# Rows of the last tile pair spread over a whole dense loop, with one block in sixteen left free, and the split of the weights written ahead of the dot

## The chip, the cores and the metric

The kernel runs on one core of one Trainium2 chip. The metric is the device time of one execution in microseconds (us); the three runs of the kernel before gave 2140.74, 2141.62 and 2150.8 us. The engines are TensorE (PE), VectorE (DVE), ScalarE (ACT), GpSimd (POOL) and the queue of SyncE (SP), which here only issues DMAs.

## The reference, cut to what matters

One decoder layer for 512 prompt tokens and 8 sample tokens. A mixer stage comes first (its output is `h`); the change does not touch it. Then comes a layer of 16384 one-neuron experts:

```python
q = einsum('td,de->te', xb, w_q)                    # 8 heads x 2 halves x 128
s = einsum('thpd,hpkd->thpk', q, keys)              # scores against 128 keys per half
s_top, i_top = top_k(s, 16)                         # the best 16 of each half
best, sel = top_k(all 16 x 16 sums, 16)             # 16 experts per token and head
gate = softmax(best)
act  = gelu(einsum('td,thkd->thk', xb, u_tab[eidx]))
out  = einsum('thk,thkd->td', gate * act, v_tab[eidx])
```

The result is added to `h` and normalised.

## The kernel before

The tokens form four tiles of 128 (t = 0 to 3) and one of 8 sample tokens. For each token of a tile 8 x 16 = 128 experts are needed; fetching "row p" means fetching, for each of the 128 partitions, that token's p-th expert with one indirect DMA. There are two ways to get the activations.

**The paired way** (tile 0 and the sample tokens, rows p = 0 to 135; `HK` = 128 rows of tile 0, then 8 sample rows, `PAIRS` = 136). POOL's `gather_pair(p)` fetches U and V of the expert together (8 KB per partition, 1 MB in all) into a ring of `RING` = 7 slots. DVE's `dot(p)` multiplies U by x and sums. ACT's `row(p)` applies Gelu and the gate to the 128 sums. Then V is added: for tile 0 by DVE's `add_vector(p)` into `ex_fin`, for sample rows by PE's `add_row(p)`. The slot is free after that.

**The dense way** (tiles 1 to 3). PE multiplies all of U by x in 128 "z" blocks of 128 experts; 16 "q" blocks make the queries. These 144 blocks (`expert_blocks`: blocks 0 to 112 are seven units of 16 blocks, of which the first and the fourth are q blocks, then z blocks alone) form the **dense loop**. In step i of it:

- SP loads block i+3 (512 KB) into one of three buffers `ex_w_raw` once the `lower` of block i is done, and stores the finished z block i-1 to `value_rows` in DRAM.
- ACT does `activate(i-1)` (Gelu out of PSUM into `ex_z_rows`; for q blocks two `take`), which waits for PE's block i-1; then `upper(i+2)` (the high half `ex_w_hi` of the weights), which waits for the load; then `row(p)`, which waits for `dot(p)`; in one step of a unit also `weight(u)` (an Exp, for which the activation table is changed twice).
- DVE does `dot(p)`, then `lower(i+2)` (the low half `ex_w_lo` = raw - high), which waits for `upper(i+2)`, then `add_vector(p-1)`, which waits for `row(p-1)`. In four steps of a unit (9, 11, 13, 15) it also does a quarter of `retrieve`, the two top-k of the next unit.
- PE does block i with 24 (z) or 48 (q) matmuls once `lower(i)` is done, and behind it `add_row` of a sample row, if there is one.

Each engine runs its list in the order in which it is written, and the engines meet only at semaphores. Row p stands in step p + `ROWS_FROM` = p + 8, so rows 0 to 135 fill steps 8 to 143, one in each.

Behind the dense loop the **value phase** handles 384 rows of tiles 1 to 3. `gather_value` fetches from `value_rows` (V beside the activations) through `VALUES` = 10 slots that lie on top of the seven pair slots: its first gather waits for all pair gathers ahead of it on POOL's queue, for the last store of `value_rows`, and for the pair rows in the slots below it. DVE's `picked` forms a diagonal of coefficients and PE's `add_row` adds V; a quarter of the rows goes through DVE's `add_vector`. Ahead of the first `picked` DVE has `scale(0)`, which waits for ACT's `root(0)`, and `normalise`.

Of the kernel before, what the change touches and what calls it, by code (L numbers as in the profile page):

```python
# [60 lines left out]
TOPK = 16  # L61
# [5 lines left out]
HK = PH * TOPK  # L67
# [6 lines left out]
WROW = D + BT  # L74
VALUE_SLOT = D + 2 * P
VALUES = 10
ROWS_FROM = 8
SPREADS = 6
PARTS_AT = (1, 4, 7, 10)
VECTOR_LAST = 1  # L80
# [1751 lines left out]
def experts(k, a, o, x_hi, x_lo, x_first, h_store, again, q, keys, keysT, h_tok, gains_row, h_out, uv_row):  # L1832
# [10 lines left out]
    PAIRS = HK + PER_ROW  # L1843
# [7 lines left out]
    blocks = expert_blocks()  # L1851
# [2 lines left out]
    by_vector = {*range(HK), *(rests - late), *range(SLOTS - VECTOR_LAST, SLOTS)}  # L1854
    rows_upto = lambda p, kind: sum((m in by_vector) == kind for m in range(p))
    on_tensor, on_vector = ([rows_upto(p, kind) for p in range(SLOTS + 1)] for kind in (False, True))
    retrieve_at, scores_at, weight_at, normalise_at = unit_schedule(SAMPLE)
    with ExitStack() as ctx:
        sb = lambda n, s, dt=F32: k.sb("ex_" + n, s, dt, ctx)
# [102 lines left out]
        with nc.Block() as block:  # L1962
# [120 lines left out]
            def _(pe):  # L2083
# [89 lines left out]
                for i, (kind, n) in enumerate(blocks):  # L2173
                    if kind == "q":
                        queries(i, n)
                    else:
                        activities(i, n)
                    if i in scores_at:
                        scores(scores_at[i])
                    if HK <= i - ROWS_FROM - 1 < PAIRS:  # L2180
                        add_row(i - ROWS_FROM - 1)
                for p in range(len(blocks) - ROWS_FROM - 1, PAIRS):
                    add_row(p)
                scores(PH + 2)
                for p in range(PAIRS, SLOTS):
# [7 lines left out]
            def _(act):  # L2193
# [86 lines left out]
                for i, (kind, n) in enumerate(blocks):  # L2280
                    if i and blocks[i - 1][0] == "z":
                        activate(blocks[i - 1][1])
                    elif i:
                        take(blocks[i - 1][1], 0)
                        take(blocks[i - 1][1], 1)
                    if i and i + 2 < len(blocks):
                        upper(i + 2)
                    if 0 <= i - ROWS_FROM < PAIRS:
                        row(i - ROWS_FROM)
                    if i in weight_at:  # L2290
                        weight(weight_at[i])
                activate(NE // P - 1)
                for p in range(len(blocks) - ROWS_FROM, PAIRS):
                    row(p)
                root(0)
                root(1)
# [10 lines left out]
            def _(dve):  # L2307
# [61 lines left out]
                def dot(p):  # L2369
                    n = order[p]  # L2370
                    if p == HK:
                        dve.wait_ge(x_in, 16 * NS)
                    dve.wait_ge(pair_loaded[p % RING], 16 * (p // RING + 1))
                    u = uv_row[:, p % RING, 0:D]
                    x = x_first[:, :] if n < HK else x_rep
                    dve.tensor_tensor_reduce(u, u, x, 1.0, 0.0, ALU.mult, ALU.add, coef[:, n:n + 1]).then_inc(dotted, 1)  # L2376
# [88 lines left out]
                lower_x(4)  # L2465
                retrieve(0)
                for i in range(len(blocks)):
                    p = i - ROWS_FROM
                    if 0 <= p < PAIRS:
                        dot(p)  # L2470
                    if 5 <= i + 2 < len(blocks) and by_dve(i + 2):
                        lower(dve, i + 2)
                    if 0 < p <= HK:
                        add_vector(p - 1)
                    if p == HK:
                        add(0)
                    if i in retrieve_at:
                        retrieve(*retrieve_at[i])
                    if i in normalise_at:
                        normalise(normalise_at[i])  # L2480
                for p in range(len(blocks) - ROWS_FROM, PAIRS):
                    dot(p)
                scale(0)
                normalise(PH + 1)
                for p in range(PAIRS, SLOTS):
# [144 lines left out]
```

## Time and profile before

| | |
|---|---|
| median of three runs | 2141.62 us (2140.74 to 2150.8) |
| the profiled execution | 2143.07 us, its span 2141.0 us |
| busy over the span | PE 90%, DVE 63%, ACT 29%, POOL 32% |
| dense loop, last activation of a z block | 1531.45 us |
| value phase, first gather | 1535.00 us |

The profile is of one execution on this core. The page gives busy shares over the whole span. The timeline has one line per instruction: start, duration, engine, line, what is written from what, and in brackets how long the engine sat idle before it and what ended that. The windows view gives busy time of each engine in a stretch, the granted clock of PE, the busy share of the DMA engines and what they moved.

### The profile page before, as it was taken

The numbers are of one execution on the slowest core, as the hardware profiler recorded it, in microseconds if no ns is written. First come the engines' busy times: TensorE is split into PE (matmuls) and PEld (weight loads), VectorE is DVE, ScalarE is ACT, GpSimd is POOL, SyncE is SP. The second block draws the span as 40 slices with busy tenths as digits, with TensorE's granted clock in tenths as the row PEclk, the third lists the DMA queues.
The fourth block names the chain that finished last, engine by engine and source line by source line (L and its number), as shares of the span: only waits on it lengthen the run. The fifth ranks groups of instructions, "written<-read, shape, count | busy, mean of one in ns | idle before, by whom it ended". The sixth has DMA issues, their size and how long they took to land.

```text
span 2141.0 us, 29757 instructions
## 1 busy us (share of the span) xinstructions
PE 1934.9 (90%) x10912; PEld 1564.2 (73%) x10912; DVE 1358.9 (63%) x2860; ACT 616.4 (29%) x1217; POOL 675.5 (32%) x556
## 2 busy tenths in 40 slices
PE   5998889988996988999999999998899998999886
PEld 4997889978966988998999999998544433434332
DVE  3219263353345535488988888988377777776663
ACT  4223312252224324444445444445300000000000
POOL 0003012100000000232333233232277776776663
PEclk9999899988998999999999999999999999999999
DMA  3557158637614573899999999999499999999997
GB/s 117 197 198 220 31 180 260 216 86 257 237 41 178 177 261 119 318 366 349 403 388 361 388 394 357 376 364 376 184 412 403 404 407 412 397 398 415 405 414 290
DMA packets 244650, 629.25 MB, mean 294 GB/s; under 512 B 19714, under 2 KB 137541, under 8 KB 226712
## 3 DMA queue, kind: packets, MB, share of 16 engines
q0 software_dynamic: 74880, 377.52, 44.5%
q1 hardware_dynamic: 169632, 249.92, 34.4%
q8 instruction: 83, 1.36, 0.2%
q14 instruction: 55, 0.45, 0.1%
HBM read 584.36 MB, written 110.21 MB: 324 GB/s over the span
## 4 chain that ended last, share of the span: by engine, by line
DMA 19%; PE 15%; DVE 14%; issue 7%; ACT 2%; POOL 2%; SPq 1%; DVEq 1%; another core or an unknown queue 0%; ACTq 0%; POOLq 0%
DMA ex_w_raw<-in_peer_ut 10%; DMA ex_uv_row<-value_rows,ex_eidx 9%; PE ps L2137 9%; DVE ex_fin L2388 4%; DVE ex_w_lo L1935 3%; POOL ex_uv_row L2066 2%; PE ps L589 2%; PE ps L590 2%; PE ps L591 2%; DVE ex_uv_row L2376 2%; ACT ex_w_hi L2199 1%; DVE ex_q_s L2401 1%; DVE ex_top_i L2335 0%; SPq L1989 0%; DVEq L162 0%
## 5 line engine op out<-in xcount | busy, mean ns | idle before, releaser
L2137 PE MATMUL ps<-ex_uv_row,ex_q_s 128*128 128x512 f32 (+1 forms) x1208 | 542.4, 599 | 61.3 <-DVE ex_q_s L2401 47.3
L2137 PEld LDWEIGHTS ps<-ex_uv_row,ex_q_s 128*128 128x128 f32 (+1 forms) x1208 | 217.1, 187 | 366.3 <-issue 347.6
L2066 POOL DMA_INDIRECT ex_uv_row<-value_rows,ex_eidx x384 | 405.2, 1055 | 214.6 <-issue 102.2
L589 PE MATMUL ps<-x_hi,ex_w_lo 128*128 128x384 f32 (+2 forms) x1296 | 427.6, 330 | 27.8 <-DVE ex_w_lo L1935 22.6
L590 PE MATMUL ps<-x_lo,ex_w_hi 128*128 128x384 f32 (+2 forms) x1296 | 423.6, 327 | 0.0
L591 PE MATMUL ps<-x_hi,ex_w_hi 128*128 128x384 f32 (+2 forms) x1296 | 423.5, 327 | 0.0
L2050 POOL DMA_INDIRECT ex_uv_row<-in_peer_uv,ex_eidx x128 | 190.6, 1489 | 410.2 <-DVE ex_fin L2388 404.7
L2388 DVE SCALAR_TENSOR_TENSOR ex_fin<-ex_uv_row,ret_tables,ex_fin 128x1024 f32<-128x1024 f32 x218 | 278.7, 1279 | 0.3
L589 PEld LDWEIGHTS ps<-x_hi,ex_w_lo 128*128 128x128 f32 x1296 | 244.6, 189 | 40.7 <-DVE ex_w_lo L1935 30.7
L591 PEld LDWEIGHTS ps<-x_hi,ex_w_hi 128*128 128x128 f32 x1296 | 245.0, 189 | 0.0
L590 PEld LDWEIGHTS ps<-x_lo,ex_w_hi 128*128 128x128 f32 x1296 | 244.8, 189 | 0.0
L1935 DVE TENSOR_TENSOR ex_w_lo<-ex_w_raw,ex_w_hi 128x1024 fp32r<-128x1024 f32 x141 | 172.3, 1222 | 102.0 <-ACT ex_w_hi L2199 93.3
L2199 ACT ACTIVATE ex_w_hi<-ex_w_raw 128x1024 fp32r<-128x1024 f32 x144 | 152.4, 1058 | 168.2 <-DMA ex_w_raw<-in_peer_ut 153.1
L2401 DVE SCALAR_TENSOR_TENSOR ex_q_s<-ex_uv_row,ret_tables,square 128x128 f32<-128x128 f32 x294 | 100.1, 352 | 90.0 <-DMA ex_uv_row<-value_rows,ex_eidx 41.7
L2376 DVE CUSTOM_DVE_ANT_0 ex_uv_row<-ex_uv_row,x_first 128x1024 f32<-128x1024 f32 x128 | 156.1, 1220 | 1.5 <-DVE ex_eidx L2361 0.3
L2217 ACT ACTIVATE ret_tables<-ex_best,ex_shift 128x16 f32<-128x16 f32 (+1 forms) x33 | 10.2, 308 | 483.6 <-DVE ex_eidx L2361 460.0
L589 PE MATMUL ps<-proj_b_whi,x_lo 128*128 128x256 f32 (+1 forms) x320 | 90.9, 284 | 7.8 <-DVE proj_b_wlo L498 7.0
L591 PE MATMUL ps<-proj_b_whi,x_hi 128*128 128x256 f32 (+1 forms) x320 | 90.6, 283 | 0.0
L590 PE MATMUL ps<-proj_b_wlo,x_hi 128*128 128x256 f32 (+1 forms) x320 | 90.4, 283 | 0.0
L643 POOL TENSOR_TENSOR dp_w_lo<-dp_w_raw,dp_w_hi 128x1024 fp32r<-128x1024 f32 x14 | 33.9, 2427 | 171.5 <-ACT dp_w_hi L669 171.5
L1935 POOL TENSOR_TENSOR ex_w_lo<-ex_w_raw,ex_w_hi 128x1024 fp32r<-128x1024 f32 x3 | 7.1, 2379 | 243.9 <-ACT ex_w_hi L2199 243.9
L2212 ACT ACTIVATE ex_z_rows<-ps 128x384 f32<-128x384 f32 x128 | 63.0, 492 | 39.4 <-PE ps L591 36.0
(415 smaller groups left out, 3418.5 us busy)
## 6 DMA issues: line engine op xcount, KB each, us to landing
value_rows<-in_peer_uv SPq DMA_DIRECT2D x64, 1024.0 KB
ex_w_raw<-in_peer_ut SPq DMA_DIRECT2D x128, 512.0 KB
value_rows<-ex_z_rows SPq DMA_DIRECT2D x128, 128.0 KB
first_raw<-in_w_in SPq DMA_DIRECT2D x8, 1024.0 KB, 7.9
ex_w_raw<-in_peer_wq SPq DMA_DIRECT2D x16, 512.0 KB
value_rows<-ex_z_rows SPq DMA_DIRECT2D x128, 64.0 KB
dp_w_raw<-in_w_in SPq DMA_DIRECT2D x14, 512.0 KB
ex_uv_row<-value_rows,ex_eidx POOLq DMA_INDIRECT x384
```

The source lines that it names most:

```text
L589: pe.matmul(out, left(llo, c), right(rhi, c), start=(c == 0), stop=False)
L590: pe.matmul(out, left(lhi, c), right(rlo, c), start=False, stop=False)
L591: ins = pe.matmul(out, left(lhi, c), right(rhi, c), start=False, stop=(c == kc - 1))
L1935: eng.tensor_tensor(w_lo[b][:, :, :], w_raw[b][:, :, :], w_hi[b][:, :, :].bitcast(F32), ALU.subtract).then_inc(split_v if by_dve(i) else s ...
L2050: pool.indirect_dma_start(uv_row[:, p % RING, :], None, a["peer_uv"][0], bass.IndirectOffsetOnAxis(ap=index, axis=0)).then_inc(pair_loaded ...
L2066: pool.indirect_dma_start(value_slot(p)[0], None, k.value_rows, bass.IndirectOffsetOnAxis(ap=eidx[:, u, n % TOPK:n % TOPK + 1], axis=0), e ...
L2137: ins = pe.matmul(k.pv[j % 2][0:r, c, :], spread[:, on_tensor[p] % SPREADS, 0:r], v[:, c * 512:(c + 1) * 512], start=first, stop=last)
L2199: act.activation(w_hi[b][:, :, :], w_raw[b][:, :, :], ACT.Copy).then_inc(rounded, 1)
L2212: act.activation(z_rows[:, b % DEEP, :], k.pb[b % 2][:, 0:BT], ACT.Gelu).then_inc(z_made, 1)
L2376: dve.tensor_tensor_reduce(u, u, x, 1.0, 0.0, ALU.mult, ALU.add, coef[:, n:n + 1]).then_inc(dotted, 1)
L2388: dve.scalar_tensor_tensor(fin[:, j % 2, :], v, coef[:, n:n + 1], fin[:, j % 2, :], ALU.mult, ALU.add).then_inc(vector_done, 1)
L2401: dve.scalar_tensor_tensor(spread[:, on_tensor[p] % SPREADS, :], z, gate_of(n), k.eye, ALU.mult, ALU.mult).then_inc(diagonal, 1)
```

## The change

It does four things. `ROWS_FROM` goes from 8 to 6. Steps 16, 32, ... 128 get no row (`row_at` maps a step to its row), so 130 rows stand in the loop and rows 130 to 135 behind it; of the sample rows PE adds only row 128 in the loop's last step and rows 129 to 135 behind it. Inside a DVE step `lower(i+2)` now comes ahead of `dot(p)`. The loops behind the dense loop start at `beside` = 130, with guards for cases in which tile 0's rows would reach that far.

```diff
-ROWS_FROM = 8
+ROWS_FROM = 6
...
+    row_at = dict(zip((i for i in range(ROWS_FROM, len(blocks)) if i % TOPK), range(PAIRS)))
+    beside = len(row_at)
...
-                    if HK <= i - ROWS_FROM - 1 < PAIRS:
-                        add_row(i - ROWS_FROM - 1)
-                for p in range(len(blocks) - ROWS_FROM - 1, PAIRS):
+                    if row_at.get(i, 0) > HK:
+                        add_row(row_at[i] - 1)
+                for p in range(max(HK, beside - 1), PAIRS):
                     add_row(p)
...
-                    if 0 <= i - ROWS_FROM < PAIRS:
-                        row(i - ROWS_FROM)
+                    if i in row_at:
+                        row(row_at[i])
...
-                for p in range(len(blocks) - ROWS_FROM, PAIRS):
+                for p in range(beside, PAIRS):
                     row(p)
...
-                    p = i - ROWS_FROM
-                    if 0 <= p < PAIRS:
-                        dot(p)
+                    p = row_at.get(i, -1)
                     if 5 <= i + 2 < len(blocks) and by_dve(i + 2):
                         lower(dve, i + 2)
+                    if p >= 0:
+                        dot(p)
                     if 0 < p <= HK:
                         add_vector(p - 1)
...
-                for p in range(len(blocks) - ROWS_FROM, PAIRS):
+                for p in range(beside, PAIRS):
                     dot(p)
+                    if p <= HK:
+                        add_vector(p - 1)
+                    if p == HK:
+                        add(0)
                 scale(0)
```

DVE's list in the middle of the dense loop before. L2376 is `dot`, L1935 `lower`, L2388 `add_vector`, L2353 and on the last quarter of `retrieve`:

```order
L2376 ISA ex_uv_row,ret_tables<-ex_uv_row,x_first 128x1024
L2376 ISA ret_tables 128x1
L1935 TENSOR_TENSOR ex_w_lo<-ex_w_raw,ex_w_hi 128x1024
L2388 SCALAR_TENSOR_TENSOR ex_fin<-ex_uv_row,ret_tables,ex_fin 128x1024
L2353 TENSOR_SCALAR ex_pick<-ex_sel 128x16
```

The same place now (the lines are two further down: L1937 `lower`, L2378 `dot`, L2390 `add_vector`; L2346 is the third quarter of `retrieve`):

```order
L1937 TENSOR_TENSOR ex_w_lo<-ex_w_raw,ex_w_hi 128x1024
L2378 ISA ex_uv_row,ret_tables<-ex_uv_row,x_first 128x1024
L2378 ISA ret_tables 128x1
L2390 SCALAR_TENSOR_TENSOR ex_fin<-ex_uv_row,ret_tables,ex_fin 128x1024
L2346 MAX ex_best<-ex_cand 128x8
```

`lower` and `dot` have changed places; ACT's list of a step (`activate`, `upper`, `row`) is as it was.

DVE's list at the end of the dense loop before, from its last `lower`; L2434 and L2435 are `scale(0)`:

```order
L1935 TENSOR_TENSOR ex_w_lo<-ex_w_raw,ex_w_hi 128x1024
L2376 ISA ex_uv_row,ret_tables<-ex_uv_row,ex_x_rep 128x1024
L2376 ISA ret_tables 128x1
L2376 ISA ex_uv_row,ret_tables<-ex_uv_row,ex_x_rep 128x1024
L2376 ISA ret_tables 128x1
L2434 RECIPROCAL ex_ms<-ex_ms 128x1
L2435 SCALAR_TENSOR_TENSOR ex_fin<-ex_fin,ex_ms,ex_w_raw 128x1024
```

And now, from its last `lower` on (x_first is the x of tile 0, ex_x_rep that of the sample rows; six more dots follow before `scale(0)`):

```order
L1937 TENSOR_TENSOR ex_w_lo<-ex_w_raw,ex_w_hi 128x1024
L2378 ISA ex_uv_row,ret_tables<-ex_uv_row,x_first 128x1024
L2378 ISA ret_tables 128x1
L2390 SCALAR_TENSOR_TENSOR ex_fin<-ex_uv_row,ret_tables,ex_fin 128x1024
L2378 ISA ex_uv_row,ret_tables<-ex_uv_row,ex_x_rep 128x1024
L2378 ISA ret_tables 128x1
L2390 SCALAR_TENSOR_TENSOR ex_fin<-ex_uv_row,ret_tables,ex_fin 128x1024
L2378 ISA ex_uv_row,ret_tables<-ex_uv_row,ex_x_rep 128x1024
L2378 ISA ret_tables 128x1
```

Where two dots followed the last `lower`, nine do now, and the last rows of tile 0 are added there too.

PE's list at that place before, and then now (L2137 and L2139 are `add_row`, two matmuls for each row; L2108 and L2110 are the scores of the next unit):

```order
L590 MATMUL ps<-x_lo,ex_w_hi 128x384
L591 MATMUL ps<-x_hi,ex_w_hi 128x384
L2137 MATMUL ps<-ex_uv_row,ex_q_s 8x512 x4
L2108 MATMUL ps<-keysT,q 128x128 x2
L2137 MATMUL ps<-ex_uv_row,ex_q_s 128x512 x30
```

```order
L590 MATMUL ps<-x_lo,ex_w_hi 128x384
L591 MATMUL ps<-x_hi,ex_w_hi 128x384
L2139 MATMUL ps<-ex_uv_row,ex_q_s 8x512 x16
L2110 MATMUL ps<-keysT,q 128x128 x2
L2139 MATMUL ps<-ex_uv_row,ex_q_s 128x512 x30
```

Six of the sample rows that PE had between blocks 137 and 143 now stand behind block 143, which makes eight there with the two that stood there before.

## Rows read from the trace of the kernel before

**Rows 1.** Windows: stretch, its length, busy us of each engine, clock, DMA share, GB/s.

```profile
937.10:1382.00 444.90, 431.71 (x2620) 426.78 (x2619) 387.21 (x600) 210.04 (x432) 144.94 (x97) 1.00 1.00 378
...
1535.00:2141.00 606.00, 534.86 (x1264) 226.84 (x1264) 429.85 (x1349) 22.48 (x63) 405.23 (x384) 0.99 0.99 394
```

**Rows 2.** Waits from 929 to 1531: who waited for whom, us in total, times, longest.

```profile
ACT ex_w_hi L2199 <- DMA ex_w_raw<-in_peer_ut: 133.7, 65, 6.7
ACT ret_tables L2224 <- DVE ret_tables L2376: 132.3, 78, 4.2
```

**Rows 3.** Timeline of ACT: `activate` of blocks 7, 17, 113 and 143.

```profile
887.97 0.48 ACT L2212 ACTIVATE ex_z_rows<-ps 128x384 f32<-128x384 f32 x1
...
937.09 0.49 ACT L2212 ACTIVATE ex_z_rows<-ps 128x384 f32<-128x384 f32 x1
...
1382.01 0.49 ACT L2212 ACTIVATE ex_z_rows<-ps 128x384 f32<-128x384 f32 x1
...
1531.45 0.49 ACT L2212 ACTIVATE ex_z_rows<-ps 128x384 f32<-128x384 f32 x1 [4.98 <-PE ps L591]
```

**Rows 4.** Timeline of DVE, two steps without retrieval.

```profile
1151.58 1.22 DVE L1935 TENSOR_TENSOR ex_w_lo<-ex_w_raw,ex_w_hi 128x1024 fp32r<-128x1024 f32 x1
1152.72 1.28 DVE L2388 SCALAR_TENSOR_TENSOR ex_fin<-ex_uv_row,ret_tables,ex_fin 128x1024 f32<-128x1024 f32 x1
1153.92 1.22 DVE L2376 CUSTOM_DVE_ANT_0 ex_uv_row<-ex_uv_row,x_first 128x1024 f32<-128x1024 f32 x1
...
1157.39 1.22 DVE L2376 CUSTOM_DVE_ANT_0 ex_uv_row<-ex_uv_row,x_first 128x1024 f32<-128x1024 f32 x1
...
1160.20 1.22 DVE L1935 TENSOR_TENSOR ex_w_lo<-ex_w_raw,ex_w_hi 128x1024 fp32r<-128x1024 f32 x1 [1.59 <-ACT ex_w_hi L2199]
```

**Rows 5.** Timeline of ACT in the same steps: `row`, `activate`, `upper`.

```profile
1151.70 0.20 ACT L2224 ACTIVATE ret_tables<-ret_tables 128x1 f32<-128x1 f32 x1 [3.97 <-DVE ret_tables L2376]
...
1152.26 0.49 ACT L2212 ACTIVATE ex_z_rows<-ps 128x384 f32<-128x384 f32 x1
1152.65 1.05 ACT L2199 ACTIVATE ex_w_hi<-ex_w_raw 128x1024 fp32r<-128x1024 f32 x1
...
1155.17 0.20 ACT L2224 ACTIVATE ret_tables<-ret_tables 128x1 f32<-128x1 f32 x1 [1.48 <-DVE ret_tables L2376]
...
1158.73 0.49 ACT L2212 ACTIVATE ex_z_rows<-ps 128x384 f32<-128x384 f32 x1
1159.12 1.05 ACT L2199 ACTIVATE ex_w_hi<-ex_w_raw 128x1024 fp32r<-128x1024 f32 x1
```

**Rows 6.** Timeline of DVE: `dot` at the ends of eight steps, four with retrieval.

```profile
1190.86 1.22 DVE L2376 CUSTOM_DVE_ANT_0 ex_uv_row<-ex_uv_row,x_first 128x1024 f32<-128x1024 f32 x1
...
1228.14 1.22 DVE L2376 CUSTOM_DVE_ANT_0 ex_uv_row<-ex_uv_row,x_first 128x1024 f32<-128x1024 f32 x1
```

**Rows 7.** Timeline of PE: two matmuls of a z block, three apart; a sample row.

```profile
1149.90 0.34 PE L589 MATMUL ps<-x_hi,ex_w_lo 128*128 128x384 f32 x1
...
1150.43 0.34 PE L589 MATMUL ps<-x_hi,ex_w_lo 128*128 128x384 f32 x1
...
1494.03 1.88 PE L2137 MATMUL ps<-ex_uv_row,ex_q_s 128*8 128x512 f32 x4
```

**Rows 8.** Timeline of SP and ACT: a load's issue, and the `upper` that waited for it.

```profile
1194.38 0.60 SPq L1983 DMA_DIRECT2D ex_w_raw<-in_peer_ut  x1
...
1205.21 1.06 ACT L2199 ACTIVATE ex_w_hi<-ex_w_raw 128x1024 fp32r<-128x1024 f32 x1 [2.95 <-DMA ex_w_raw<-in_peer_ut]
```

**Rows 9.** Timeline at the start of the value phase: `root(0)`, first gather, `normalise`, first `picked`.

```profile
1531.84 1.02 ACT L2238 ACTIVATE ps<-ex_fin 128x1024 f32<-128x1024 f32 x1
...
1535.00 1.98 POOL L2066 DMA_INDIRECT ex_uv_row<-value_rows,ex_eidx  x1 [37.76 <-PE ps L2137]
...
1536.28 0.23 DVE L2408 TENSOR_SCALAR ret_tables<-ret_tables,ex_tot 128x16 f32<-128x16 f32 x1
...
1541.92 0.35 DVE L2401 SCALAR_TENSOR_TENSOR ex_q_s<-ex_uv_row,ret_tables,square 128x128 f32<-128x128 f32 x1 [5.40 <-DMA ex_uv_row<-value_rows,ex_eidx]
```

## Prediction, made before the changed kernel ran

> **What bounds the kernel now.** I read the windows first, to see what a stretch is short of. The value phase lasts 606 us with the DMA engines at 0.99 and 394 GB/s [rows 1]: 384 rows in 606 us, 1.58 us each. Nothing in it changes, so it only starts earlier or later. What is left is the dense loop, up to the last `activate` at 1531.45 [rows 3]. In its six steady units of 16 blocks, from block 17 (937.09) to block 113 (1382.01), a unit takes 444.92 / 6 = **74.15 us** [rows 3]. In that stretch PE is busy 431.7 of 444.9 us, DVE 387.2, and the DMA share is 1.00 at 378 GB/s [rows 1]. So three resources are nearly full, and the waits say who waits for whom: ACT waits 133.7 us for loads of U and 132.3 us for the dot product [rows 2]. The period is thus set by how the lists of ACT and DVE mesh, with loads that come just late. That is where the change acts.
>
> **How a step runs now.** A plain DVE step is `dot` to `dot`, 1157.39 - 1153.92 = 3.47 us [rows 4]. A z block on PE takes 24 matmuls at (1150.43 - 1149.90) / 3 = 0.177 us, 4.2 us [rows 7]. With the dot first, `dot(p)` of a step is done while ACT still works on `upper(i+2)`: ACT finds it ready, goes on to `activate(i)`, and DVE's `lower` fits in beside that. A loop that goes from a dot through ACT to the next `lower` and back covers two steps, so it doesn't bind.
>
> **The order inside the step, the main term.** Now `lower(i+2)` stands ahead of `dot(p)`, on an engine that takes its list in order, and ACT's list is unchanged. That closes a ring of one step, every link of which waits for the last:
>
> - `activate(i-1)` to `upper(i+2)`: 1152.65 - 1152.26 = 0.39 [rows 5]
> - `upper` to `lower`: 1160.20 - 1159.12 = 1.08 [rows 4, 5]
> - `lower` to the next DVE instruction, now the dot: 1152.72 - 1151.58 = 1.14 [rows 4]
> - dot to ACT's `row`: 1155.17 - 1153.92 = 1.25 [rows 4, 5]
> - `row` to the next `activate`: 1152.26 - 1151.70 = 0.56 [rows 5]
>
> Together **4.42 us**. No step with a row can be shorter, whatever PE (4.2) and DVE (3.47) could do. `add_vector`, behind the dot, is beside it. What is lost with it: DVE falls behind in retrieval steps and today catches up at 3.47 us a step; now it can't. What is queued behind the waiting `lower` is the dot, and ACT waits for that.
>
> The retrieval steps stay DVE's own. Eight steps, four with retrieval, took 1228.14 - 1190.86 = 37.28 us [rows 6]; less four plain ones (13.9) and about 0.4 of waiting for `upper` leaves 22.9 us for the four. The step with `weight` adds the table changes to the ring: 1158.73 - 1155.17 = 3.56 from `row` to `activate` instead of 0.56 [rows 5], so 3.0 more, 7.4 us.
>
> **The step without a row.** It has no dot in its ring, so it could be as short as 0.39 + 1.08 = 1.5 us if PE is ahead and the load is in, and as long as a PE block, 4.2 us, if not. Nothing in the trace shows such a step in the middle. I take the middle, 2.9.
>
> **A unit now**: 10 plain steps 44.2, four retrieval steps 22.9, `weight` step 7.4, free step 2.9, and 0.7, an estimate for two q blocks, whose eviction is two instructions of a z block's kind. That is **78.1 us** (76.7 to 79.4 by the free step), against 74.15: +3.9 in each of six units, **+23.6** (+15.3 to +31.5).
>
> **The first and the last part.** From block 7 to 17 before: 937.09 - 887.97 = 49.1 us [rows 3]. Now 4 x 4.42 + 22.9 + 7.4 + 2.9 = 50.9: **+1.8** (+0.4 to +3.1). The two rows that move into steps 6 and 7 lie beside blocks where PE is the slower one and cost nothing; if not, 0.5 us. From block 113 to 143 before: 1531.45 - 1382.01 = 149.4 us [rows 3]. Now 11 retrieval steps (two full sets and one without its first quarter, about 63.1), three `weight` steps 22.2, a free step 2.9, 15 plain ones 66.3: 154.5, **+5.0** (+3.7 to +6.3). In it lies the gain of the moved sample rows: before, six blocks at the end carried 1.88 us of PE each [rows 7], 11.3 us. That time comes back only as far as the ring and the retrievals of steps 134 to 140 leave it, and these rows then run while the last store and the first value gathers are under way.
>
> **The tail.** Let X be the end of the last block. The value gathers still need the last store, 1535.00 - 1531.45 = 3.55 us after X [rows 3, 9]. POOL's gather of row 135 waits for row 128's slot, free at X + 1.9 (one sample row [rows 7]), and stands ahead of them: its 1 MB is 2.7 us at 394 GB/s. Its dot comes at about X + 1.9 + 6.9 + 1.1 = X + 9.9 (6.9 is gather to first use [rows 9], 1.1 an estimate for twice the bytes). Then dot 1.25, `row` of a sample row about 0.9, and `root(0)`, `scale(0)`, `normalise`, 1536.5 - 1531.84 = 4.7 [rows 9], all ahead of the first `picked`: X + 16.7, where it was 1541.92 - 1531.45 = 10.5. Ten value slots hold 15.8 us of transfers and hide most of these 6.2 us. I take the transfer alone, **+2.7** (0 to +6.2).
>
> **Loads.** DMA work per unit falls by one pair row of 1 MB, some 2.7 us of 74. On the other side, a load is issued after `lower` of three blocks earlier, and the ring leaves it 3 x 4.42 less `lower`, issue and `upper`, about 10.5 us; one took 1205.21 - 1194.38 = 10.8 us [rows 8]. If plain steps slip by 0.2 us for that, 79 steps give +16. If loads are in time, nothing. I take 0 for the sum and keep 16 as the upper end.
>
> The page "DMA: Bandwidth & Descriptors" of the Trainium skill, section on the anatomy of one DMA, fits a transfer as 2.0 us plus bytes over 436 GB/s. By that an estimate for a load is 3.2 us and none would ever be late; the trace doesn't agree, since [rows 8] show 10.8 us under this load. By the page the 16 us could be struck; by the row they stay.
>
> **Sum**: 23.6 + 1.8 + 5.0 + 2.7 = +33.1 us on a span of 2141.0, thus 2174.1, and 2176.2 for the profiled execution's 2143.07. The median before is 1.5 us below that execution, so against the runs I say **2175 us**. Its own range is 2161 (all low ends: +19.4) to 2205 (all high ends, +47, and the late loads, +16).
>
> **Rivals.**
> *Faster: loads and DVE were the limit, the order doesn't bind.* ACT's 133.7 us of waiting for loads [rows 2] speak for it: `lower` earlier means loads issued up to 1.2 us earlier, and a sixteenth of the gathers and dots goes. A unit would fall to PE's busy time, 431.71 / 6 = 72.0 us [rows 1]; six units give -12.9, the end up to -11.3 from the sample rows, the tail +2.7: -21.5, 2120 us. It decides if the ring comes out below 4.2 us, that is if `row` is done before ACT needs to go on; against it stand ACT's 78 waits for the dot already now [rows 2]. Chance 0.14.
> *No difference.* The ring binds, but free steps are worth a whole step and sample rows come back in full: 76.7 less some 1.5 of load waits a unit, +6, the end -6: within 11 us of before, 2131 to 2152. Chance 0.11.
> *Only the tail pays.* The dense loop is as before, since DMA at a share of 1.00 [rows 1] sets it in both; then +2.7 to +6.2, 2144 to 2148. That is within 0.5% too. Chance 0.05.
> *Slower, as summed*: 0.70.
>
> **How the numbers follow.** About 0.5% (11 us) is what this kernel's measurement can tell from no change. Slower 0.70; same 0.11 + 0.05 = 0.16; faster 0.14. The range leaves out the faster case and a little above: 2142 to 2205.
>
> **What would show it.** In the profile after, steps of 4.4 us one after another where there were 3.5 and 6; `lower` always waiting for `upper`; ACT's waits for the dot grown well over 132 us, its waits for loads shrunk; PE's waits for `ex_w_lo` grown; a unit near 78 us; eight sample rows behind block 143. A unit of 72 to 73 us would say that the ring has slack that I don't see; one above 80, that loads come late in it.

## The result, and the profile after

The changed kernel takes 2194.63 us (median of four runs, 2191.4 to 2197.2) against 2141.18 us for the kernel before (2125.25 to 2150.8). The ratio is 1.0256, 95% interval 1.0193 to 1.032: slower, inside the predicted range, but with 53 us of loss where 33 were forecast. Over all its runs here the kernel before lies between 2125.3 and 2158.4 us, so a few us of any difference between two profiles mean nothing. Ratios leave out the executions in a slower state of the chip, two of the kernel before (2796 and 3446 us) and one of run 11 (2149 us).

The profiled execution spans 2195.1 us. Cutting both spans at the same `activate` instructions shows where 54.1 us went. The starts after are these (ACT's timeline; L2214 is `activate`; blocks 7, 17, 113 and 143, as in [rows 3]):

```profile
893.17 0.49 ACT L2214 ACTIVATE ex_z_rows<-ps 128x384 f32<-128x384 f32 x1
...
946.03 0.49 ACT L2214 ACTIVATE ex_z_rows<-ps 128x384 f32<-128x384 f32 x1
...
1425.57 0.49 ACT L2214 ACTIVATE ex_z_rows<-ps 128x384 f32<-128x384 f32 x1
...
1578.62 0.47 ACT L2214 ACTIVATE ex_z_rows<-ps 128x384 f32<-128x384 f32 x1
```

| part | before | after | difference | forecast |
|---|---|---|---|---|
| up to the first `upper` of the dense loop | 828.6 | 830.7 | +2.1 | 0 |
| first `upper` to block 7 | 59.4 | 62.4 | +3.0 | 0 |
| block 7 to 17 | 49.1 | 52.9 | +3.8 | +1.8 |
| six units, block 17 to 113 | 444.9 | 479.5 | +34.6 | +23.6 |
| block 113 to 143 | 149.4 | 153.1 | +3.6 | +5.0 |
| block 143 to the end | 609.5 | 616.5 | +7.0 | +2.7 |

Each part is the difference of two starts. A unit is now 479.5 / 6 = 79.9 us, against 74.15.

**The ring.** One step after, in the order of time (ACT's and DVE's timelines; L2201 is `upper`, L1937 `lower`, L2378 `dot`, L2226 and L2231 `row`):

```profile
1107.59 1.07 ACT L2201 ACTIVATE ex_w_hi<-ex_w_raw 128x1024 fp32r<-128x1024 f32 x1
...
1108.70 1.23 DVE L1937 TENSOR_TENSOR ex_w_lo<-ex_w_raw,ex_w_hi 128x1024 fp32r<-128x1024 f32 x1 [0.76 <-ACT ex_w_hi L2201]
1109.84 1.22 DVE L2378 CUSTOM_DVE_ANT_0 ex_uv_row<-ex_uv_row,x_first 128x1024 f32<-128x1024 f32 x1
...
1111.10 0.20 ACT L2226 ACTIVATE ret_tables<-ret_tables 128x1 f32<-128x1 f32 x1 [2.43 <-DVE ret_tables L2378]
1111.33 0.29 ACT L2231 ACTIVATE ret_tables<-ret_tables 128x1 f32<-128x1 f32 x1
1111.66 0.49 ACT L2214 ACTIVATE ex_z_rows<-ps 128x384 f32<-128x384 f32 x1
1112.05 1.05 ACT L2201 ACTIVATE ex_w_hi<-ex_w_raw 128x1024 fp32r<-128x1024 f32 x1
```

Start to start the links are 1.11, 1.14, 1.26, 0.56 and 0.39, together 4.46 us from one `upper` to the next, where 4.42 was worked out. Both engines idle in each round: ACT 2.43 us for the dot, DVE 0.76 us for the high half. That is how a ring looks in a timeline: two engines take turns, each waiting for the other, and neither is full.

The waits (929 to 1578 us; who waited for whom, total, times, longest) say it for the whole loop:

```profile
ACT ret_tables L2226 <- DVE ret_tables L2378: 316.9, 121, 4.1
DVE ex_w_lo L1937 <- ACT ex_w_hi L2201: 130.9, 96, 3.9
...
PE ps L589 <- ACT ex_z_rows L2214: 57.5, 46, 4.5
ACT ex_w_hi L2201 <- DMA ex_w_raw<-in_peer_ut: 42.1, 28, 4.0
```

ACT's wait for the dot went from 132.3 to 316.9 us and its wait for loads from 133.7 to 42.1 [rows 2]. Loads did come sooner relative to their need, but nothing could use that. In the windows view of the six units (columns as in [rows 1]) everything is less full than it was: PE is busy 93% of the time (97% before), DVE 79% (87%), the DMA share is 0.95 (1.00), with 338 GB/s instead of 378:

```profile
946.00:1425.60 479.60, 444.84 (x2643) 427.82 (x2642) 378.02 (x586) 206.34 (x422) 87.25 (x90) 1.00 0.95 338
```

**The free step.** Around step 48, which has no row (ACT's timeline; the first `upper` is that of block 50, the second that of block 51; step 49 behind it is the one with `weight`):

```profile
1090.69 0.49 ACT L2214 ACTIVATE ex_z_rows<-ps 128x384 f32<-128x384 f32 x1
1091.18 1.06 ACT L2201 ACTIVATE ex_w_hi<-ex_w_raw 128x1024 fp32r<-128x1024 f32 x1
1092.15 0.47 ACT L2214 ACTIVATE ex_z_rows<-ps 128x384 f32<-128x384 f32 x1
1095.51 1.06 ACT L2201 ACTIVATE ex_w_hi<-ex_w_raw 128x1024 fp32r<-128x1024 f32 x1 [2.89 <-DMA ex_w_raw<-in_peer_ut]
...
1102.56 0.49 ACT L2214 ACTIVATE ex_z_rows<-ps 128x384 f32<-128x384 f32 x1
```

From `activate` to `activate` the free step is as short as it can be, 1092.15 - 1090.69 = 1.46 us, and the next `upper` then waits 2.89 us for its load. The two steps take 1102.56 - 1090.69 = 11.9 us, 12.4 on average over the six units, where 2.9 + 7.4 = 10.3 was forecast. Why was that load late? Its buffer was free after the `lower` of block 48, but SP's list has the store of block 46 ahead of it, and that store waits for ACT's `activate` (timelines of DVE, ACT and SP; L1990 is the first half of a store, L1985 a load):

```profile
1083.29 1.23 DVE L1937 TENSOR_TENSOR ex_w_lo<-ex_w_raw,ex_w_hi 128x1024 fp32r<-128x1024 f32 x1
...
1086.25 0.49 ACT L2214 ACTIVATE ex_z_rows<-ps 128x384 f32<-128x384 f32 x1
...
1086.77 0.33 SPq L1990 DMA_DIRECT2D value_rows<-ex_z_rows  x1
...
1087.72 0.57 SPq L1985 DMA_DIRECT2D ex_w_raw<-in_peer_ut  x1
```

The `lower` ends at 1084.52 and the load goes out at 1087.72, 3.2 us later; from there to the `upper` that waits for it are 7.8 us. So the ring reaches the loads too, through the stores. The order of SP's list was not varied, so what another order would give is not shown.

**The tail.** SP, POOL and DVE behind the last block, which ends at 1578.6 (L1991 is the second half of the last store, L2052 the gather of row 135, L2068 the first value gather, L2403 the first diagonal):

```profile
1578.96 1.47 POOL L2052 DMA_INDIRECT ex_uv_row<-in_peer_uv,ex_eidx_s  x1 [1.96 <-PE ps L2139]
...
1579.84 0.51 SPq L1991 DMA_DIRECT2D value_rows<-ex_z_rows  x1
...
1588.38 1.23 DVE L2378 CUSTOM_DVE_ANT_0 ex_uv_row<-ex_uv_row,ex_x_rep 128x1024 f32<-128x1024 f32 x1 [5.42 <-DMA ex_uv_row<-in_peer_uv,ex_eidx_s]
...
1588.99 1.43 POOL L2068 DMA_INDIRECT ex_uv_row<-value_rows,ex_eidx  x1 [8.55 <-issue]
...
1595.00 0.34 DVE L2403 SCALAR_TENSOR_TENSOR ex_q_s<-ex_uv_row,ret_tables,square 128x128 f32<-128x128 f32 x1
```

The first value gather starts 10.4 us behind the last block instead of 3.55 [rows 9], 9.15 us after the last store was issued; before, that took 1535.00 - 1532.35 = 2.65 us. "issue" means that the view names no releaser. What POOL's list has there is the wait for the last stores (PE's `add_row` of row 129, whose slot the first value gather needs, was done by about 1581). The DMA engines were carrying the pair gathers of rows 133 to 135, issued at 1572.68, 1575.02 and 1578.96, and the load of the last norm's gain, issued at 1578.84: 263 GB/s from 1579.8 to 1589.0, against 73 GB/s in the same wait before.

### The profile page after: what moved, and what is told of

Same layout as the page of the kernel before. It is cut to its first block, busy times and chain, and to the rows that moved or that the text cites. A ratio compares the mean times of both kernels' runs of the same rounds, so it can differ in the third digit from the quotient of the medians.

```text
span 2195.1 us, 29758 instructions
## 1 busy us (share of the span) xinstructions
PE 1952.7 (89%) x10912; PEld 1566.8 (71%) x10912; DVE 1363.8 (62%) x2860; ACT 615.6 (28%) x1217; POOL 611.3 (28%) x556
## 4 chain that ended last, share of the span: by engine, by line
DMA 21%; DVE 12%; issue 9%; PE 9%; ACT 7%; POOL 3%; SPq 2%; DVEq 0%; another core or an unknown queue 0%; POOLq 0%
DMA ex_w_raw<-in_peer_ut 11%; DMA ex_uv_row<-value_rows,ex_eidx 10%; PE ps L2139 7%; DVE ex_uv_row L2378 5%; ACT ex_w_hi L2201 3%; POOL ex_uv_row L2068 3%; DVE ex_fin L2390 2%; ACT ret_tables L2231 1%; ACT ex_z_rows L2214 1%; DVE ex_q_s L2403 1%; SPq L1991 1%; ACT ret_tables L2226 1%; DVE ex_top_i L2337 1%; ACT L2214 1%; PE ps L589 0%
## 5 line engine op out<-in xcount | busy, mean ns | idle before, releaser
L2139 PE MATMUL ps<-ex_uv_row,ex_q_s 128*128 128x512 f32 (+1 forms) x1208 | 541.3, 599 | 59.7 <-DVE ex_q_s L2403 43.0
L589 PE MATMUL ps<-x_hi,ex_w_lo 128*128 128x384 f32 (+2 forms) x1296 | 432.9, 334 | 65.4 <-ACT ex_z_rows L2214 62.0
L2139 PEld LDWEIGHTS ps<-ex_uv_row,ex_q_s 128*128 128x128 f32 (+1 forms) x1208 | 217.4, 187 | 367.6 <-issue 351.1
L2068 POOL DMA_INDIRECT ex_uv_row<-value_rows,ex_eidx x384 | 406.2, 1058 | 184.6 <-issue 112.2
L2052 POOL DMA_INDIRECT ex_uv_row<-in_peer_uv,ex_eidx x128 | 125.1, 977 | 555.3 <-DVE ex_fin L2390 547.2
L2390 DVE SCALAR_TENSOR_TENSOR ex_fin<-ex_uv_row,ret_tables,ex_fin 128x1024 f32<-128x1024 f32 x218 | 279.1, 1280 | 0.3
L1937 DVE TENSOR_TENSOR ex_w_lo<-ex_w_raw,ex_w_hi 128x1024 fp32r<-128x1024 f32 x141 | 172.6, 1225 | 163.0 <-ACT ex_w_hi L2201 160.5
L2201 ACT ACTIVATE ex_w_hi<-ex_w_raw 128x1024 fp32r<-128x1024 f32 x144 | 152.0, 1056 | 54.1 <-DMA ex_w_raw<-in_peer_ut 53.0
L2378 DVE CUSTOM_DVE_ANT_0 ex_uv_row<-ex_uv_row,x_first 128x1024 f32<-128x1024 f32 x128 | 155.9, 1218 | 0.0
L2403 DVE SCALAR_TENSOR_TENSOR ex_q_s<-ex_uv_row,ret_tables,square 128x128 f32<-128x128 f32 x294 | 99.9, 351 | 84.5 <-DMA ex_uv_row<-value_rows,ex_eidx 37.0
L2219 ACT ACTIVATE ret_tables<-ex_best,ex_shift 128x16 f32<-128x16 f32 (+1 forms) x33 | 10.2, 308 | 483.6 <-DVE ex_eidx L2363 483.5
L2226 ACT ACTIVATE ret_tables<-ret_tables 128x1 f32<-128x1 f32 x136 | 27.5, 202 | 344.5 <-DVE ret_tables L2378 344.5
L1937 POOL TENSOR_TENSOR ex_w_lo<-ex_w_raw,ex_w_hi 128x1024 fp32r<-128x1024 f32 x3 | 7.1, 2377 | 244.4 <-ACT ex_w_hi L2201 244.4
```

The costliest lines, as they stand in the source:

```text
L589: pe.matmul(out, left(llo, c), right(rhi, c), start=(c == 0), stop=False)
L1937: eng.tensor_tensor(w_lo[b][:, :, :], w_raw[b][:, :, :], w_hi[b][:, :, :].bitcast(F32), ALU.subtract).then_inc(split_v if by_dve(i) else s ...
L2052: pool.indirect_dma_start(uv_row[:, p % RING, :], None, a["peer_uv"][0], bass.IndirectOffsetOnAxis(ap=index, axis=0)).then_inc(pair_loaded ...
L2068: pool.indirect_dma_start(value_slot(p)[0], None, k.value_rows, bass.IndirectOffsetOnAxis(ap=eidx[:, u, n % TOPK:n % TOPK + 1], axis=0), e ...
L2139: ins = pe.matmul(k.pv[j % 2][0:r, c, :], spread[:, on_tensor[p] % SPREADS, 0:r], v[:, c * 512:(c + 1) * 512], start=first, stop=last)
L2201: act.activation(w_hi[b][:, :, :], w_raw[b][:, :, :], ACT.Copy).then_inc(rounded, 1)
```

## The experiments

The theory: the order inside DVE's step closes a ring of one step, and that is the loss; the rest is the tail and rows at steps 6 and 7. Rivals: the loss comes from where the rows stand (free steps with late loads, rows behind the loop), or DVE's order is bad in itself, by what it does to gathers and loads. A run's parts are cut at the same instructions as above. The runs were made in three series, in which the kernel before had medians of 2140.4 us (runs 1 to 4), 2142.3 (5 to 8) and 2139.6 (9 to 12); each ratio is against the kernel before of its own series, so across series ratios are compared and not times.

**1. The dot first again, all else as changed.**

```diff
-                    if 5 <= i + 2 < len(blocks) and by_dve(i + 2):
-                        lower(dve, i + 2)
                     if p >= 0:
                         dot(p)
+                    if 5 <= i + 2 < len(blocks) and by_dve(i + 2):
+                        lower(dve, i + 2)
```

> The changed kernel with the dot put back ahead of the lower half; the rows stay where the change put them. The ring theory (lower, dot, ACT's row, activate, upper, each waiting for the last, 4.42 us a step) says that this alone takes the loss away: a unit of 16 blocks at 72 to 73.5 us (before 74.15, less a row's work), the dense loop some 15 us shorter than before, the tail 7 us longer, about 2130 us. The rival, that the loss comes from where the rows stand (late loads behind free steps, rows behind the loop), says 2185 us or more and a unit near 79.9 us as in the changed kernel.

2122.96 us, ratio 0.992 (0.9893 to 0.9947): the order was the whole loss, and the placing of the rows is a gain. A unit is 72.7 us, from `activate` at 933.32 and 1369.43. The waits of this run (930 to 1530 us):

```profile
ACT ret_tables L2226 <- DVE ret_tables L2378: 132.5, 71, 4.8
ACT ex_w_hi L2201 <- DMA ex_w_raw<-in_peer_ut: 99.8, 53, 6.5
DVE ex_w_lo L1937 <- ACT ex_w_hi L2201: 77.0, 46, 5.6
```

The wait for the dot is back at its old size, with loads less late than before. In its tail the first value gather starts at 10.2 us, as after the change, so the tail belongs to the rows and not to the order. The part from the first `upper` to block 7 is 59.0 us: the +3.0 there is the ring too (rows in steps 6 and 7 cost nothing with the dot first).

**2. Only the order, in the kernel before.**

```diff
+                    if 5 <= i + 2 < len(blocks) and by_dve(i + 2):
+                        lower(dve, i + 2)
                     if 0 <= p < PAIRS:
                         dot(p)
-                    if 5 <= i + 2 < len(blocks) and by_dve(i + 2):
-                        lower(dve, i + 2)
```

> The kernel before with only the order inside DVE's step changed, lower half ahead of the dot. The ring theory: a unit of 11 plain steps at 4.42, four retrieval steps 22.9, the weight step 7.4 and 0.7 for the queries, 79.7 us, six units +33, the first part +3, the last part +7 to +12, tail as before: 2185 to 2190 us. The rival that puts the loss on the placing of the rows: 2141 us, no change.

2206.3 us, ratio 1.032 (1.0299 to 1.034), a unit of 81.3 us, ACT waiting 317.6 us for the dot (930 to 1530 us). The ring alone does it; the rival of no change falls. The time is 16 us above what I expected, and a unit 1.6 us longer than the links and the retrievals add up to. The waits of this trace are enough to account for that: in the six units ACT also waits 14.4 us for loads, 2.4 us a unit, which the sum has not (19.5 us in run 4).

**3. The ring cut on ACT's side, DVE's list untouched.**

```diff
-                    if i in row_at:
-                        row(row_at[i])
+                    if i - 1 in row_at:
+                        row(row_at[i - 1])
...
-                for p in range(beside, PAIRS):
+                for p in range(beside - 1, PAIRS):
                     row(p)
```

> The changed kernel, lower half still ahead of the dot, but ACT does each row one step later, so that it no longer waits in the step for the dot of that step. The ring theory: the ring is cut although DVE's list is untouched; a unit at 72 to 74 us and 2125 to 2145 us in all. The rival that DVE's order is bad in itself (dots too late for the gathers, DVE idle at the lower half): 2180 us or more, DVE still waiting 130 us for the high half.

2126.56 us, ratio 0.9935 (0.9909 to 0.996), a unit of 73.2 us. DVE still has the lower half first and nothing is lost. So the order is not bad in itself. In the waits ACT now waits for PE and for loads, as in a loop that runs at PE's pace (waits of this run, 930 to 1530 us):

```profile
ACT ex_w_hi L2201 <- DMA ex_w_raw<-in_peer_ut: 117.9, 60, 5.4
ACT ex_z_rows L2214 <- PE ps L591: 86.3, 56, 2.4
DVE ex_w_lo L1937 <- ACT ex_w_hi L2201: 63.7, 49, 5.6
ACT ret_tables L2226 <- DVE ret_tables L2378: 49.5, 40, 6.2
```

Its tail is longer still, 14.3 us to the first value gather.

**4. No free step.** The changed kernel with `row_at = dict(zip((i for i in range(ROWS_FROM, len(blocks))), range(PAIRS)))`.

> The changed kernel with a row in every step from 6 on, so rows 0 to 135 stand in steps 6 to 141 and none behind the loop. By the ring theory with the measured 12.4 us for a free step and the one behind it against 4.42 + 7.42: a unit 79.3 us, so -4 us over six; sample rows back between PE blocks +10; tail as short as before, -7: about 2194 us. If a free step really gave 2.9 us each, as predicted, the unit would be 81 us or more and the total 2205 us.

2208.16 us, ratio 1.0322 (1.0301 to 1.0344), a unit of 82.2 us. My expectation was wrong: I had priced a step with a row at the bare ring, 4.42 + 7.42 us, but without free steps the units in these two kernels (2 and 4) take 81.3 and 82.2. A free step takes 1.4 to 2.3 us out of a unit even inside the ring. The tail is back at 3.6 us.

The place of the free step says why. Step 48, like every step that the change leaves free, stands right behind one with a quarter of `retrieve`, with DVE late from it. In run 2, where it has a row, the `upper`s around it are these (ACT's timeline, blocks 50 to 52):

```profile
1097.12 1.05 ACT L2199 ACTIVATE ex_w_hi<-ex_w_raw 128x1024 fp32r<-128x1024 f32 x1
...
1103.26 1.05 ACT L2199 ACTIVATE ex_w_hi<-ex_w_raw 128x1024 fp32r<-128x1024 f32 x1
...
1110.69 1.05 ACT L2199 ACTIVATE ex_w_hi<-ex_w_raw 128x1024 fp32r<-128x1024 f32 x1
```

With a row the step takes 6.14 us and not 4.42, and the next 7.43. After the change the same two are 1095.51 - 1091.18 = 4.33 and 7.43 us. So the free step saves about 1.8 us, the lag of DVE behind the retrieval, although it ends in a wait for a load.

**5. The same without the ring.** Dot first and no free step.

> Dot first, a row in every step from 6 on, none behind the loop: what the free steps are worth when no ring binds. Theory: a free step takes 2.5 us of DVE and 2.7 us of DMA out of a unit that both nearly fill, so without them a unit is back at 74 us (72.7 with them), the tail back at 3.6 us to the first value gather; 2130 to 2140 us. If the gain of the run with the dot first came from rows starting two steps sooner, this one is at 2123 us too.

2149.93 us, ratio 1.0028 (1.0004 to 1.0053), 10 us above the expected end, a unit of 74.6 us against 72.7 with free steps. So the free steps are what makes run 1 fast, and starting rows two steps sooner gives nothing. From this profile to that of run 1 the parts differ by -2.6 (block 7 to 17), -11.7 (six units), -7.1 (last 30 blocks, with the sample rows) and +6.5 (tail).

**6. Only ACT's row later, in the kernel before.** `row(i - 1 - ROWS_FROM)` in step i.

> The kernel before with one change: ACT does each row one step later; rows stand as before and the dot is first on DVE. If ACT's wait for the dot (132 us before) is what stretches the loop beside late loads, this alone gives a unit of 73 to 74 us and about 2130 us. If the waits only change their name because loads are late anyway, 2141 us.

2133.75 us, ratio 0.9956 (0.9934 to 0.9978), a unit of 73.0 us, without a single free step. Half a per cent for one index, and about as short a unit as run 1 has with free steps.

**7 and 8. The tail cured,** in run 3's kernel (ACT's row one step later). Two free steps (112 and 128), so that all dots and pair gathers lie in the loop, and PE's adds of rows 130 to 135 alone behind it; lower half first, then dot first.

```diff
-    row_at = dict(zip((i for i in range(ROWS_FROM, len(blocks)) if i % TOPK), range(PAIRS)))
+    row_at = dict(zip((i for i in range(ROWS_FROM, len(blocks)) if i not in (112, 128)), range(PAIRS)))
...
-                    if row_at.get(i, 0) > HK:
-                        add_row(row_at[i] - 1)
-                for p in range(max(HK, beside - 1), PAIRS):
+                    if HK + 2 <= row_at.get(i, 0) <= HK + 3:
+                        add_row(row_at[i] - 2)
+                for p in range(HK + 2, PAIRS):
                     add_row(p)
```

> Row one step later on ACT, lower half ahead of the dot, two free steps only (112 and 128), so that all dots and all pair gathers are done inside the loop; PE's adds of sample rows 130 to 135 alone stand behind it. The theory of the tail (the last store lands 8 us late because it shares the DMA engines with the last three pair gathers) says that the first value gather comes 3.6 us after the last block again, not 10 to 14, with the first diagonal at 10.5 us; with a unit of 73 to 74 us and the last 30 blocks at 135 us, 2115 to 2128 us. If PE's eight rows behind the loop made the tail long, it stays at 10 us and the total near 2130 us.

> The same with the dot ahead of the lower half. With ACT's row a step late neither order closes a ring of one step, so the ring theory expects no difference beyond 0.5% from the run with the lower half first. A rival, that the lower half ahead of the dot gets loads under way sooner, expects this one 5 us or more slower, with more waits of ACT for loads.

2134.88 us, ratio 0.9974 (0.9946 to 1.0003), and 2128.55 us, ratio 0.9941 (0.9917 to 0.9964). The tail theory holds: the first value gather comes 3.55 us behind the last block in both, with six of PE's rows still behind it. The last store and that gather of run 8:

```profile
1517.66 0.43 SPq L1991 DMA_DIRECT2D value_rows<-ex_z_rows  x1
...
1520.32 0.94 POOL L2068 DMA_INDIRECT ex_uv_row<-value_rows,ex_eidx  x1 [24.58 <-PE ps L2139]
```

The total of run 7 is 7 us above the range that I expected, and it isn't the missing free steps that cost this in the units: they take 73.3 and 73.1 us, with a free step in one of the six, where run 3 has 73.2 with all of them. The profile of run 7 is shorter than that of run 3 (2126.1 against 2131.2 us), its median ratio is larger, and the intervals overlap; which is the faster is open. The two orders have spans of 2126.1 and 2126.3 us in their profiles, so neither closes a ring. The medians lie 6.3 us apart, over ten runs each (2127.1 to 2143.4, and 2122.0 to 2133.9): within the 0.5% that the theory allows, but some three times the standard error, in favour of the dot first. Where these 0.3% would lie no trace shows.

**9. The last three pair gathers halved,** in run 1's kernel. The V half of sample rows 133 to 135 is left out.

```diff
-                    pool.indirect_dma_start(uv_row[:, p % RING, :], None, a["peer_uv"][0],
+                    pool.indirect_dma_start(uv_row[:, p % RING, 0:D if p >= PAIRS - 3 else 2 * D], None, a["peer_uv"][0],
```

> The run with the dot first, with the last three pair gathers (rows 133 to 135) fetching only the U half of each expert, 1.5 MB less in all; the V half of these sample rows is left as it was in the slot, so the sample outputs aren't the reference's. If the last store of the activations is late because it shares the DMA engines with these gathers, the first value gather comes 6 to 8 us after the last block, not 10.2. If something else holds it (PE's rows, POOL's own work), it stays at 10.

The first value gather comes at 8.3 us (10.2 in run 1); store to gather takes 1522.62 - 1515.55 = 7.1 us instead of 1524.68 - 1515.66 = 9.0:

```profile
1515.55 0.45 SPq L1991 DMA_DIRECT2D value_rows<-ex_z_rows  x1
...
1522.62 0.94 POOL L2068 DMA_INDIRECT ex_uv_row<-value_rows,ex_eidx  x1 [7.58 <-PE ps L2139]
```

1.5 MB less bring it forward by 1.9 us. The releaser named here is PE, but PE's row for that slot had been done by about 1516; the same wait is called "issue" in run 1. This is one profile, and the same wait with all bytes is 9.15 us after the change and 8.4 in run 12, so the gain is 1.3 to 2.1 us. The other side agrees: in runs 3 and 10, where the last pair gather is issued 1.1 to 1.2 us behind that store and not ahead of it, the wait is 13.1 and 12.4 us. A rival remains for a part of it. The load of the gain (L2028, 128 partitions of 4 KB) is issued about 1 us ahead of the last store in runs 1, 9, 12 and after the change, but 3.2 us or more ahead of it in every kernel with a short tail. No run separates the two; run 9 leaves the gain's load as it was and still has 7.1 us.

**10. Both cuts of the ring,** dot first and ACT's row one step later, with the eight free steps.

> The changed kernel with the dot ahead of the lower half and ACT's row one step later: both cuts of the ring at once, with the eight free steps. If each cut already frees the loop, a unit stays at 72.5 to 73.3 us and the total at 2118 to 2130 us, the tail 10 to 14 us. If the two add up, a unit at PE's 71.5 us and about 2112 us.

2122.33 us, ratio 0.9895 (0.9831 to 0.9958), a unit of 73.0 us: one cut frees the loop, the second adds nothing to a unit. Nor do the free steps here: run 6 has none and the same unit, 73.0. What they still bring is in the last 30 blocks, 134.0 us against 148.6 in run 6, where the sample rows leave PE's list; the tail takes back 9.6 of it (13.3 us to the first value gather). Together with run 1 it is the best kernel here, about 1% ahead of the kernel before.

**11. Five free steps, three rows behind the loop.** Dot first, free steps 16, 48, 80, 112 and 128, PE's adds as in run 7.

> Dot first, five free steps (16, 48, 80, 112, 128) in place of eight, PE's adds of rows 128 and 129 in the loop and six behind it, so that only rows 133 to 135 have their dots behind the loop and their gathers go out some 5 us sooner. Theory: three free steps fewer cost about 8 us at 2.5 us each, the tail gives 3 to 6 us back (first value gather 4 to 7 us after the last block): 2122 to 2132 us. If free steps are worth less than the tail, it beats the run with the dot first (2123 us).

2130.09 us, ratio 0.9936 (0.9898 to 0.9973). The first value gather is at 3.56 us, a unit 73.0 us, the span 2127.0. The total falls where the theory put it and can't be told from run 1's, but the parts do not bear the theory out. The three free steps fewer in the six units cost 1.8 us against run 1's profile and not 7.5, the tail gives 5.4 us and the last 30 blocks 7.6; this profile began the dense loop 6.7 us later. Nine of its ten runs scatter from 2115.3 to 2138.8 us, which hides more than any of these.

**12. The free step moved to the table change,** 17, 33, ... 129, dot first (`if i % TOPK != 1`).

> Dot first, the free step one step later in each unit (17, 33, ... 129), in the step in which ACT changes its table. If ACT is what lasts longest in that step, its row (0.56 us and a wait for the dot) is best left out there and a unit is 0.5 to 1 us shorter than 72.7, about 2118 us. If the free step serves DVE behind its retrieval steps, later is worse: a unit near 73.5 us and 2128 us.

2133.57 us, ratio 0.9956 (0.9917 to 0.9995), a unit of 73.2 us. Neither expectation can be called met: the unit isn't shorter than 72.7, and no clear loss against run 1 shows either, since the intervals overlap.

## Why the prediction was right, and where it was mis-sized

**The main step held.** "That closes a ring of one step", 4.42 us: the timeline shows 4.46, and runs 1, 2 and 3 show that the ring is the cause, by opening it on either engine and by closing it alone. Of the signs listed ahead all but one appeared: steps of 4.43 to 4.46 us, `lower` waiting for `upper` (130.9 us, in 96 of 126 steps, so often and not always), ACT's waits for the dot far over 132 (316.9), waits for loads down (42.1), eight sample rows behind block 143. The unit was 79.9 us, near the 80 above which I had put late loads. The sign that failed: PE's waits for `ex_w_lo` nearly vanished, from 21 to 1.7 us over the dense loop; PE now waits for ACT's `activate` instead (57.5 us). The lower half was in time; what came late was the PSUM bank that PE needs back.

**How much of it was luck.** The loss is 1.6 times the one forecast. None of the four terms of the sum lies in its own range: +34.6 us in the six units against +15.3 to +31.5, +3.8 in the first part against +0.4 to +3.1, +7.0 in the tail against 0 to +6.2, and, a little short, +3.6 in the last part against +3.7 to +6.3. The time lies in the range all the same, since the range had 16 us more for plain steps that slip by late loads. Loads were late, but elsewhere: of 34.3 us of waiting for them in the six units, 19.8 lie behind the free steps, and the fourteen other steps of a unit came out at their forecast, waits and all. What filled the range were terms sized too small, which make 21.0 us together: +2.1 ahead of the loop, +3.0 at its start, +2.0 to block 17, +11.0 in the six units, -1.4 in the last blocks, +4.3 in the tail.

**The term of the free step was mis-sized.** I took 2.9 us for it and 7.4 for the next. Measured from `activate` to `activate` they are 1.5 and 10.8 us on average, or 4.3 and 7.5 from `upper` to `upper`. I priced the free step apart from the loads, but it makes the next `upper` meet a late one, by 2.7 to 3.7 us in each of the six units. My sum for a load, issued right after the `lower` three blocks earlier, was wrong there: the store ahead of it in SP's list held it for another 3.2 us. That is +2.1 us; the other fourteen steps sum to 67.5, where 67.8 was forecast, so a unit exceeds its forecast by 1.8 (79.9 against 78.1). Over six units that is 11 us of the 21 by which the profile exceeds the sum. Yet free steps pay as long as ACT's `row` waits for the dot of its own step: 1.4 to 2.3 us a unit with the ring (runs 2, 4 and the changed kernel), 1.9 with the dot first (runs 1, 5).

With the row one step later they pay nothing in the units, which the series was not made to ask but shows:

| free steps in the six units | row one step later | a unit |
|---|---|---|
| none | run 6 | 73.0 |
| one | runs 7, 8 | 73.3, 73.1 |
| six | runs 3, 10 | 73.2, 73.0 |

Single units of one trace scatter far more than these means (from 69.1 to 78.5 us in run 1), so a few tenths between them say nothing; runs 1 and 9, whose loops are the same up to the last gathers, have 72.7 and 72.8.

**The start.** "The two rows that move into steps 6 and 7 ... cost nothing" was wrong by 3.0 us. I held them against PE's blocks alone, but the ring ties them to the loads, and behind a `lower` that waited 8.4 us for the `upper` of block 8 (a wait of 9.6 us before, with nothing behind it) now stood the dot. With the dot first the same rows cost nothing (run 1). The blocks behind it, +3.8 instead of +1.8, I did not take apart.

**The tail was mis-sized, 7.0 instead of 2.7.** The step that failed is "the value gathers still need the last store, 3.55 us after X". The chain of DVE and ACT was right: the first diagonal was forecast at X + 16.7 and came at 16.4. But the last store shares the DMA engines with the last pair gathers and took 9.15 us to release POOL instead of 2.65. Run 9 shows that their bytes matter, runs 7, 8 and 11 that the delay is gone when they go out sooner. How much of it belongs to the gain's load, which also lies there, is open.

**The loads.** Late loads cost 42.1 us of waiting after the change, in waits up to 4.0 us, and 19.8 us of that lie in the steps behind the six free steps. The load behind free step 48 took 7.8 us from issue to use. The Trainium skill's fit ("DMA: Bandwidth & Descriptors", anatomy of one DMA), which the page gives for DMAs issued by GpSimd, while these are issued by SP, makes an estimate of 3.2 us for 512 KB, by which no load would be late. The traces disagree again.

**The rival of a gain** (2120 us) is what the change gives without its order: run 1 measures 2123, a unit of 72.7 where the rival had 72.0. That the totals agree is in part chance: against the profile before, run 1's has -8.8 us in the six units, -4.4 in the last blocks and +6.6 in the tail, where the rival had -12.9, -11.3 and +2.7. The rival's own point of decision, whether the ring stays under PE's block, decided against it by 0.3 us a step.

**What stays open.** 2.1 us of the difference lie ahead of the dense loop, where nothing was changed; the fourteen profiles here reach their first `upper` between 824.4 and 833.5 us, so that is scatter. Why the last 30 blocks took 1.4 us less than forecast I did not ask. Untried are another order of loads and stores in SP's list, and the gain's load moved out of the tail. And I did not try free steps with gathers that are sent out sooner without giving up free steps, for which more slots would be needed.

## What to carry to other kernels

When two engines pass work back and forth in one step, follow the chain from one instruction to itself in the next step and add its links start to start; if it closes within one step, that sum is a floor on the step, however idle the engines are. Swapping two instructions of a list can close such a ring (here +3% of the whole kernel), and moving the consumer one step later opens it again at no cost in the loop. Look for such a wait before you make room: a free slot in a full loop gave 1.4 to 2.3 us of some 75 to 82 while ACT waited for the dot of its own step, and nothing once it did not. And work that a free slot pushes behind the loop is paid for where its transfers meet the last stores.

## What the runs showed that was not expected

POOL's pair gathers took 0.98 us each after the change where they took 1.49 before (page, costliest groups; the group of before has 190.6 us for the same 128):

```profile
L2052 POOL DMA_INDIRECT ex_uv_row<-in_peer_uv,ex_eidx x128 | 125.1, 977 | 555.3 <-DVE ex_fin L2390 547.2
```

The bytes are the same. In the changed kernel DVE's next instruction behind `add_vector`, which releases the gather, is often a `lower` that still has to wait; that POOL is quicker beside an idle DVE is a guess from this. With the dot first and free steps a gather takes 1.43 us again (130.22 us for 91 in the six units of run 1). Over the six units all kernels fall into three groups by what stands behind `add_vector` in DVE's list: 0.97 us where it is a `lower` in the ring (runs 2, 4 and the changed kernel), 1.20 us where it is a `lower` without the ring (runs 3 and 7), 1.44 to 1.52 us where it is a dot (all others). That fits the guess and does not prove it, since the duration of a POOL instruction is rough in this profile. It cost nothing here, since POOL is not what the loop waits for.

The last store, two DMAs of 64 and 128 KB, took 2.65 us from the issue of its second half to releasing its waiter with the DMA engines moving 73 GB/s, which is little more than the store itself. It took 7.1 us with some 1.5 MB of gathers and the gain's load beside it, 8.4 to 9.2 us with some 3 MB of gathers, and 12.4 to 13.1 us when the last gather came behind it.
